# Two-network kernel on one core: the last ple panel into other banks, p split earlier, squares added in pairs

## The reference, cut to what matters

```python
merged = ga * (ya @ w_a) + gb * (yb @ w_b) + gc * (yc @ w_c)   # g*: sigmoid(x @ w_m + b_m), split in three
out = merged @ w_o
r = ALPHA * x + out
r = r + jax.nn.sigmoid(r @ w_pg) * (p_i @ w_p)
return _layernorm(r, ln_g, ln_b)
...
mu = jnp.mean(xf, axis=-1, keepdims=True)
var = jnp.mean(jnp.square(xf - mu), axis=-1, keepdims=True)
y = (xf - mu) * lax.rsqrt(var + NORM_EPS)
```

## Time and profile before

| | |
|---|---|
| three runs | 1935.71, 1938.17, 1938.35 us, median 1938.17 |
| profiled execution | 1930.44 us, span 1929.0 us |
| mean granted TensorE clock | 0.976 of full |
| PE busy | 1844.3 us, 96% of the span |
| DVE busy | 1325.3 us, 69% |
| ACT busy | 959.4 us, 50% |
| memory traffic | 389.69 MB, mean 202 GB/s |

### The profile page before, as it was taken

The page is one execution under the profiler, slowest core; times in us unless marked ns, Lnnn a source line. Parts: engine busy times, 40 slices in busy tenths (PEclk is TensorE's granted clock), DMA queues, the critical chain, the costliest instruction groups (busy, mean ns, idle before and its releaser), DMA issues.

```text
span 1929.0 us, 34207 instructions
## 1 busy us (share of the span) xinstructions
PE 1844.3 (96%) x15080; PEld 1778.8 (92%) x15080; DVE 1325.3 (69%) x1799; ACT 959.4 (50%) x1322; POOL 61.4 (3%) x76
## 2 busy tenths in 40 slices
PE   7999988999999998999999999999999999999998
PEld 7988988899989897999999899999999999899998
DVE  5667776765776777766677757667766677867664
ACT  5465554445655545534456335445544456345443
POOL 0000100000001001000000000001000000010000
PEclk9999999889999998999899999999999899999998
DMA  8445355463463554566555344665566455345662
GB/s 313 175 169 225 145 212 197 167 262 133 179 253 123 207 192 190 201 252 255 205 200 228 142 153 167 249 262 221 201 254 257 183 219 234 116 153 175 246 259 107
DMA packets 59283, 389.69 MB, mean 202 GB/s; under 512 B 6656, under 2 KB 9472, under 8 KB 15232
## 3 DMA queue, kind: packets, MB, share of 16 engines
q1 hardware_dynamic: 59136, 387.52, 53.1%
HBM read 386.45 MB, written 1.05 MB: 201 GB/s over the span
## 4 chain that ended last, share of the span: by engine, by line
PE 65%; DVE 22%; ACT 11%; DMA 1%; issue 1%; SPq 0%; DVEq 0%; ACTq 0%
PE banks L781 16%; PE banks L782 15%; PE banks L783 15%; DVE weights_split L929 9%; ACT weights_split L923 5%; PE bank L782 4%; PE bank L783 4%; PE bank L781 4%; DVE weights L909 2%; ACT map L1364 1%; DMA weights<-in_weights 1%; DVE xbc L2379 1%; ACT map L1370 1%; DVE map_stat L1552 1%; PE bank L849 1%
## 5 line engine op out<-in xcount | busy, mean ns | idle before, releaser
L929 DVE TENSOR_TENSOR weights_split<-weights,weights_split 128x2048 fp32r<-128x2048 f32 (+3 forms) x306 | 656.5, 2147 | 340.5 <-ACT weights_split L923 339.4
L923 ACT CAST weights_split<-weights 128x2048 fp32r<-128x2048 f32 (+3 forms) x306 | 542.5, 1776 | 94.3 <-PE bank L783 70.3
L781 PE MATMUL banks<-u,weights_split 128*128 128x256 f32 (+1 forms) x1648 | 462.0, 280 | 7.2 <-DVE weights_split L929 3.9
L782 PE MATMUL banks<-u,weights_split 128*128 128x256 f32 (+1 forms) x1648 | 457.7, 278 | 0.0
L783 PE MATMUL banks<-u,weights_split 128*128 128x256 f32 (+1 forms) x1648 | 457.6, 278 | 0.0
L781 PE MATMUL banks<-x,weights_split 128*128 128x256 f32 x1056 | 303.0, 287 | 23.3 <-DVE weights_split L929 10.0
L781 PEld LDWEIGHTS banks<-u,weights_split 128*128 128x128 f32 (+1 forms) x1648 | 309.5, 188 | 10.2 <-DVE u L2483 4.3
L782 PEld LDWEIGHTS banks<-u,weights_split 128*128 128x128 f32 (+1 forms) x1648 | 309.7, 188 | 0.4
L783 PEld LDWEIGHTS banks<-u,weights_split 128*128 128x128 f32 (+1 forms) x1648 | 309.6, 188 | 0.4
L782 PE MATMUL banks<-x,weights_split 128*128 128x256 f32 x1056 | 296.5, 281 | 0.0
L783 PE MATMUL banks<-x,weights_split 128*128 128x256 f32 x1056 | 296.5, 281 | 0.0
(11 more groups left out here) (331 smaller groups left out, 3041.1 us busy)
## 6 DMA issues: line engine op xcount, KB each, us to landing
weights<-in_weights SPq DMA_DIRECT2D x262, 1024.0 KB, 6.5
weights<-in_ada SPq DMA_DIRECT2D x80, 1024.0 KB, 4.8
weights<-in_weights SPq DMA_DIRECT2D x36, 512.0 KB, 5.3
weights<-in_weights SPq DMA_DIRECT2D x4, 576.0 KB, 5.6
constants_second<-in_constants_second SPq DMA_DIRECT2D x1, 1792.0 KB, 8.6
weights<-in_weights SPq DMA_DIRECT2D x2, 640.0 KB, 7.4
h<-in_x SPq DMA_DIRECT2D x2, 512.0 KB, 5.0
out<-xbc SPq DMA_DIRECT2D x4, 256.0 KB, 2.2
```

What stands on the lines that cost most here:

```text
L781: pe.matmul(out, left[0], right[0], start=start, stop=False, **more)
L782: pe.matmul(out, left[0], right[1], start=False, stop=False, **more)
L923: act.do.copy(split[:, 0, 0:n], raw[:, 0:n]).then_inc(*self.act_wrote.inc(("weights", key)))
L929: dve.do.tensor_tensor(split[:, 1, 0:n], raw[:, 0:n], split[:, 0, 0:n].bitcast(F32), ALU.subtract).then_inc(*self.dve_wrote.inc(("weights" ...
```

## The change

Three edits, each once per layer of the first network.

- The step `split_p` stands ahead of gate_b 0 and 1, no longer between gate_b 1 and ple 0. The load of `p` is put into SP's list one head earlier.
- The two banks of ple 1 come from the ring `turned` and no longer from `products`.
- After the 8 subtractions of the mean, DVE adds the squares of chunks 1, 3, 5, 7 to those of 0, 2, 4, 6, in place, and PE sums 4 chunks with 8 matmuls, no longer 8 chunks with 16.

```diff
@@ fill() of first_layer
             yield from self.dense("b_z", l, range(2))
             yield from merge("c", ("ycn", l))
+            self.add("split_p", l)
             yield from self.dense("gate_b", l, [0, 1])
-            self.add("split_p", l)
             self.run(self.dense("ple", l, [0], 2))
@@ head()
-                if h == HEADS - 3:
+                if h == HEADS - 4:
                     self.loads.append(("p", l))
@@ Program
+    def bank_ring(self, key):
+        return self.turned if key[0] == "ple" and key[2] == 1 else self.products
+
     def tensor_rows(self, key, b, x, x_from=0, x_marks=None):
-        bank = self.products.take(("bank", key, b))
-        pe.wait_ge(*self.products.free(("bank", key, b)))
+        bank = self.bank_ring(key).take(("bank", key, b))
+        pe.wait_ge(*self.bank_ring(key).free(("bank", key, b)))
@@ norm_of
+        if name == "ln":
+            return b["merged"][:, 0:DC:2, :], 1, DC // 2, D, 1e-5, self.turned, [
+                (self.dve_wrote, ("squares", tag, c)) for c in range(0, DC, 2)]
@@ vector_first, "mean"
+                for c in range(0, DC, 2):
+                    dve.wait_ge(self.act_wrote, ("squares", ("ln", l), c + 1))
+                    dve.do.tensor_tensor(b["merged"][:, c, :], b["merged"][:, c, :], b["merged"][:, c + 1, :],
+                                         ALU.add).then_inc(*self.dve_wrote.inc(("squares", ("ln", l), c)))
```

More of the change, by code:

```diff
@@ L832, in norm_of @@
             return b["square_sum"], 1, 1, D, 1e-6, ring, [(self.pool_wrote, ("square_sum", tag))]
-        ring, eps = (self.turned, 1e-5) if name == "ln" else (self.values, 1e-6)
-        return (b["merged"] if name == "ln" else b["squares"], 1, DC, D, eps, ring,
-                [(self.act_wrote, ("squares", tag, c)) for c in range(DC)])
+        if name == "ln":
+            return b["merged"][:, 0:DC:2, :], 1, DC // 2, D, 1e-5, self.turned, [
+                (self.dve_wrote, ("squares", tag, c)) for c in range(0, DC, 2)]
+        return b["squares"], 1, DC, D, 1e-6, self.values, [(self.act_wrote, ("squares", tag, c)) for c in range(DC)]
     def tensor_norm(self, tag, part):
@@ L946, in scalar_copy @@
         act, name, n = self.act, ("bank", key, b), min(2, self.panels[key][2] // P - 2 * b)
-        bank = self.products.tile(name)
+        bank = self.bank_ring(key).tile(name)
         act.wait_ge(self.filled, name)
@@ L950, in scalar_copy @@
             *self.act_wrote.inc(name))
-        self.products.emptied(name, self.act_wrote, name)
+        self.bank_ring(key).emptied(name, self.act_wrote, name)
     def scalar_tokens(self, key, dst):
```

## The result

| | before | changed |
|---|---|---|
| runs | 4, 1934.41 to 1938.35 us | 4, 1918.55 to 1921.07 us |
| median | 1936.94 us | 1920.6 us |
| ratio | | 0.9917, 95% interval 0.9905 to 0.9928 |
| profiled execution | 1930.44 us, span 1929.0 | 1921.07 us, span 1919.6 |
| mean granted clock | 0.976 | 0.976 |

The change takes 16.1 us off (1936.94 x 0.0083; 13.9 to 18.4 by the interval).

What follows compares the result with a forecast made beforehand. The prediction took PE, busy for 96% of the span, to bound the kernel. Its terms, -7.9 - 6.9 + 0.3 = -14.5 us, took the median from 1938.2 to 1923.7 us, range 1917.5 to 1929.5.

Steps and rivals of the forecast that it cites:

- -1.5: Behind the first layer's wait ahead of ple 0: 3.1 us of work at half clock takes half, -1.5 us.
- 24 x 4.00/38: Ahead of gate_b 2: a ple panel's 24 matmuls, put at 2.8 us, in finding 1.8 us of cover for its weights.
- 325.08 - 2.14 - 321.32: At ple 1: its second bank's time, put at 1.5 us, so that w_out 0 starts at 321.0.
- the two small stalls: New PE stalls: about 0.2 us within w_out 0 for splits of `merged`, 0.3 us ahead of w_out 1 for weights.
- What PE wants next does not come earlier: Behind ple 1: none of what PE wants next hung on its stall, so 0.5 us per layer is given back.
- ple 1's gain is given back in w_out: Rival: in w_out PE waits for late splits of `merged` and panel roundings; -10.7 us, 1927.5 us, chance 0.14.
- the first rival: All waits go and the clock holds in the layer norms; -18.9 us, 1919.3 us, chance 0.13.
- the fourth rival: Slower than before: the layer norm's stop leaves PE at 1.2 GHz for following dense panels; +5.5 us, 1943.7 us, chance 0.02.
- I take the same difference off both: Whole kernel: the -14.5 us summed on the profiled execution, 1930.4 us, is also taken off the median, 1938.2 us.

Runs made afterwards that it cites:

- e5_order: The changed kernel with a new order around ple 1: the last two splits of `merged` put behind ple 1; 1918.69 us, ratio 0.9909 to the kernel before.
- interleaved pairs: The changed kernel with each addition of squares put among the mean's subtractions, no longer behind all eight; 1920.9 us, ratio 0.9920 to the kernel before.

## Why the prediction was right, and where not

The forecast was -14.5 us and 1923.7 us; measured were -16.1 (-13.9 to -18.4) and 1920.6 us. The mechanism of edit 1 was right, that of edit 2 missed a step, and the total is good in part by luck. Edit 2 gave 4.4 us less than its term. Against that stand edit 1 with 2.2 us more, edit 3 with 0.9 us more, and 2.9 us by which the three together give more than their sum. Only the first of these four lies clear of the noise.

**Edit 1, forecast -7.9, measured -10.1 alone.** The mechanism was right at each step: p's split fits ahead of the roundings, ple 0's weights and banks are there, nothing takes over. The term that looks too small is the clock, "-1.5", which counted one fall of the clock in two waits because the profile showed one. There were falls at 7 of 8 such waits. A fall costs half of the time that PE works in it: from 292.65 to 296.0 and from 672.82 to 678.3 in the second profile of before, so 1.7 and 2.7 us, and 1.5 to 2.9 us over all seven. As an estimate, two waits of 3.04 us and 1.75 falls of 1.94 us, the means over the eight waits and the seven falls, are 9.5. The times alone don't settle it, as 7.9 and 10.1 both lie in the interval. Two slips in its working change nothing: 24 x 4.00/38 is 2.5 us and not 2.8 (a ple panel took 2.94 in all), and in edit 2 325.08 - 2.14 - 321.32 is 1.6 and not 1.5.

**Edit 2, forecast -6.9, measured -2.5 alone.** This is the step that failed. Both waits went, and the two small stalls came within 0.1 us of their 0.2 and 0.3 (0.14 and 0.20, with 0.22 more ahead of w_out 0). What was missed is that w_out's products feed a chain that PE needs again at ple_gate 0. "What PE wants next does not come earlier" was checked for weights and for the splits of `merged`, but only as far as w_out 2; the residual's chain has PE's own period, and it could move forward only by the 1.18 us that it had waited for PE. It starts 3.1 us later against w_out 0 than before. It gives back 2.05 and 2.07 us, and in 5 of 10 layers with this stop (changed, edit 2 alone, and the changed kernel without pairs, interleaved or with the old load) the clock fell behind it. `e5_order` shows it: with the chain started 1.9 us earlier the stop is 0.48 us. The rival "ple 1's gain is given back in w_out" had the right idea at the wrong place: not the panels' weights but the products' way back. By the table the way from ple 1 to the mean is 1.2 and 2.0 us shorter in the changed kernel than in the profile that the forecast was made against; in the second of these PE's slower panels of before (5.65 us) have a part.

**Edit 3, forecast +0.3, measured -0.6 alone, and nothing in the pair of kernels with and without.** The stop of 3.2 us (3.17) and 3.4 us for 16 records at 1.2 GHz (3.57) were right in the second layer; in the first the clock held and the sums took 1.95, as the first rival had it, but it fell right behind them. Behind each layer norm PE works at 1.2 GHz for a while, before and after: until 392.5 and 767.9 before, from 375.4 and 750.9 on; until 386.8 and 758.8 now, from 373.1 and 741.8 on. So the fourth rival, more slow work behind the norm, did not come. Over all layers the way from mean to factors is 7.60 us without pairs (12 layers) and 7.51 with them behind the subtractions (8 layers). PE has half the matmuls and waits longer for them.

**The clock.** The prediction took one profile's falls for the kernel's. The Trainium skill (TensorE: Matmul & The Clock Gate, What's actually happening) says that recent activity decides the throttle, and that the same kernel shows a different number of slow matmuls from run to run. The runs agree: the same program had 0.976 and 0.969. The Trainium skill (the same page and section) puts the ramp penalty at under 1% of a span for modelling. No run here has that penalty by itself, but the same program differs by 9.9 us or 0.5% between two executions, which is more than what edits 2 and 3 are worth.

Falls also got rarer with the change, which the forecast had only at ple 0. Averaged over executions, the mean clock of the changed kernel is 0.9762 (4 executions). Against the kernel before on the same chip it is 0.9752 to 0.9712 without the pairs, 0.9740 to 0.9712 with interleaved pairs, and 0.9752 to 0.9720 with the old load; but 0.9740 to 0.9727 with edit 1 alone and 0.9721 to 0.9727 with edit 2 alone. At 1.2 us for each 0.001, the 0.003 to 0.004 of both edits together are an estimated 3 to 5 us of the 16.1. The forecast had 1.5.

**Why the profiles differ by less than the runs.** The profiled executions differ by 9.4 us and the medians by 16 because the execution of before that was profiled kept its clock behind one wait for `p` and both pairs at ple 1, and lay 6.5 us under its median, while the changed kernel's lay at its own. "I take the same difference off both" was the assumption here, and it did not hold.

**What stays open.** The three edits alone add up to 13.2 us, and together they gave 16.1 and, without pairs, 16.9. The intervals cover the difference. What decides whether the clock falls at a given stop was not settled. Nor is what interleaved pairs are worth: the timelines say 0.5 us a layer over plain ones, while the runs say +0.6 without the new order (0.9917 to 0.9920) and -2.8 with it (1918.69 to 1915.93), and -3.5 against no pairs at all (1917.41 to 1913.87), all within their intervals.

## What to carry to other kernels

- When a wait is removed, follow the work that then starts earlier to the next place where its results come back. If the chain in between has about the consumer's own period, it makes up nothing of a late start, and what it lacks is paid at that place (2.05 us of 3.95 here).
- A wait of a few us costs its length and, often, a stretch at half clock behind it; take that from several executions, whose mean clocks are cheap to compare. One profile shows one draw.
- Halving an engine's work at a join gained nothing here (7.60 and 7.51 us), because the additions that halve it stand on the same critical path.

## What the runs showed of the hardware

- Stops of TensorE as short as 1.78 us were followed by 1.2 GHz in some executions (704.50 in the second profile of before, low from 705.6 on; 2.08 us in edit 2 alone), and one of 3.10 us was not.
- The mean granted clock differs between executions of the same program (0.969 to 0.975 in 47 of them), and the time follows it, some 1.2 us for each 0.001.
- 16 records of plain fp32 with one moving column take 1.95 us at 2.4 GHz and 3.57 us at 1.2 GHz.
- A fall of the clock moves as well as it goes. In the first profile of before it fell behind the stop of 2.21 us that ends at 248.12, and PE then waited 0.88 us at the next join (273.22). In the changed kernel it held behind the same stop (248.22), PE came early to that join and stood there for 2.30 us, and the clock fell there; the second profile of before did the same (2.30 us). So part of what a fall costs is slack that would have been waited away.
